# Seven block products in place of eight in the second input half of the second feed-forward parts

## The reference

```
def swiglu(x, w_in, w_out):
    gate, up = jnp.split(x @ w_in, 2, axis=-1)
    return (jax.nn.silu(gate) * up) @ w_out

x = x + 0.5 * swiglu(rmsnorm(x, p['ffn2_norm'][i]), p['ffn2_w_in'][i], p['ffn2_w_out'][i])
```

## Time and profile before

| | us |
|---|---|
| median of 3 runs (2357.9 to 2358.71) | 2358.68 |
| profiled execution, span from first to last instruction | 2357.9 |
| PE busy in it | 2332.7 |
| DVE busy | 1295.9 |
| ACT busy | 869.0 |
| POOL busy | 609.4 |

### The profile page before, as it was taken

How to read it: one execution, slowest core, us unless ns; L and a number is a source line. 1 busy time by engine, 2 the same in 40 slices (tenths; PEclk the granted TensorE clock), 3 DMA queues, 4 the chain that set the end, 5 groups by cost and what they waited for, 6 DMA issues and landing times.

```text
span 2357.9 us, 50146 instructions
## 1 busy us (share of the span) xinstructions
PE 2332.7 (99%) x21043; PEld 2270.3 (96%) x21043; DVE 1295.9 (55%) x1906; ACT 869.0 (37%) x1399; POOL 609.4 (26%) x591
## 2 busy tenths in 40 slices
PE   8999999999999999999999999999999999999999
PEld 8999999889979999999999999999999979999999
DVE  6653643964576443445543344577777666443443
ACT  4422333453233321322433233267775233321323
POOL 4779967331103000004111010432122102000003
PEclk9999999999999999999999999999999999999999
DMA  6455445553562333333543333233332653333332
GB/s 167 128 161 149 123 134 169 171 170 107 166 242 84 98 99 91 96 96 99 158 117 111 100 108 115 83 100 108 104 111 77 213 188 91 97 94 94 98 94 94
DMA packets 483707, 289.19 MB, mean 123 GB/s; under 512 B 22289, under 2 KB 466962, under 8 KB 482514
## 3 DMA queue, kind: packets, MB, share of 16 engines
q1 hardware_dynamic: 477856, 280.66, 40.4%
q0 software_dynamic: 560, 1.84, 0.6%
q10 hardware_dynamic: 5122, 4.25, 0.5%
HBM read 258.86 MB, written 27.85 MB: 122 GB/s over the span
## 4 chain that ended last, share of the span: by engine, by line
PE 90%; DVE 4%; POOL 2%; ACT 1%; issue 1%; DMA 1%; SPq 0%; DVEq 0%; POOLq 0%; ACTq 0%
PE lin L3021 51%; PE lin L3026 25%; PE mis L2512 4%; POOL sTmp L737 1%; PE mis L2650 1%; PE lin L2600 1%; PE lin L2762 1%; PE mis L2633 1%; PE lin L2757 1%; PE lin L2983 1%; POOL sGe L738 0%; DVE w_lo L1827 0%; POOL sFe L738 0%; PE lin L2650 0%; PE mis L2626 0%
## 5 line engine op out<-in xcount | busy, mean ns | idle before, releaser
L1827 DVE TENSOR_TENSOR w_lo<-raw,w_hi 128x1024 fp32r<-128x1024 f32 (+1 forms) x322 | 464.0, 1441 | 294.4 <-ACT w_hi L1330 293.7
L1330 ACT ACTIVATE w_hi<-raw 128x1024 fp32r<-128x1024 f32 (+1 forms) x328 | 365.1, 1113 | 314.2 <-PE lin L3026 244.4
L3021 PE MATMUL lin<-a_rear,w_hi 128*128 128x264 f32 x3552 | 455.6, 279 | 0.0
L3021 PE MATMUL lin<-a_front,w_hi 128*128 128x256 f32 x3552 | 451.5, 279 | 1.1 <-DVE a_rear L1840 0.7
L3021 PEld LDWEIGHTS lin<-a_rear,w_hi 128*128 128x128 f32 x3552 | 432.6, 188 | 0.0
L3021 PEld LDWEIGHTS lin<-a_front,w_hi 128*128 128x128 f32 x3552 | 424.4, 188 | 4.5 <-issue 1.8
L3026 PE MATMUL lin<-a_rear,w_lo 128*128 128x264 f32 x1776 | 245.1, 278 | 0.0
L3026 PE MATMUL lin<-a_front,w_lo 128*128 128x256 f32 x1776 | 240.5, 277 | 1.0 <-DVE w_lo L1827 1.0
L2391 DVE SCALAR_TENSOR_TENSOR xT<-lin,xT 128x520 f32<-128x520 f32 (+1 forms) x87 | 60.9, 700 | 322.8 <-PE lin L3026 322.1
L1063 POOL TENSOR_TENSOR acc<-xT 128x520 f32<-128x520 f32 x8 | 12.2, 1521 | 864.6 <-DVE xT L2391 836.6
L3026 PEld LDWEIGHTS lin<-a_rear,w_lo 128*128 128x128 f32 x1776 | 223.8, 188 | 0.0
(11 more groups left out here) (512 smaller groups left out, 3181.5 us busy)
## 6 DMA issues: line engine op xcount, KB each, us to landing
raw<-in_ffn_w_in_dram SPq DMA_DIRECT2D x176, 512.0 KB, 3.9
raw<-in_ffn_w_out_dram SPq DMA_DIRECT2D x64, 704.0 KB, 4.6
kc<-in_cache_mem_k_dram SPq DMA_DIRECT2D x32, 512.0 KB, 7.1
vc<-in_cache_mem_v_dram SPq DMA_DIRECT2D x16, 1024.0 KB, 9.1
raw<-in_hg_w_in_dram SPq DMA_DIRECT2D x32, 512.0 KB, 4.3
raw<-in_xattn_w_kv_dram SPq DMA_DIRECT2D x16, 512.0 KB, 4.4
raw<-in_s_w_glu_dram SPq DMA_DIRECT2D x16, 512.0 KB, 4.0
raw<-in_xattn_w_q_dram SPq DMA_DIRECT2D x16, 512.0 KB, 3.9
```

The costliest lines, as they stand in the source:

```text
L1330: act.activation(w_hi[:, j, 0:kt, :], raw[:, j, 0:kt, :], ACT.Copy).then_inc(hi_ready, 1)
L1827: dve.tensor_tensor(low_weights(n, j), raw[:, j, 0:kt, :], w_hi[:, j, 0:kt, :].bitcast(F32), ALU.subtract).then_inc(lo_ready, 1)
L3021: pe.matmul(lpart(j, half), high[:, k, :], (x_lo if u else x_hi)[half][:, k, :], start=start and u == 0 and k == 0, stop=False)
```

## The change

The input product of ffn2_in1 in both layers is computed by Winograd's form of Strassen's scheme. For one hidden tile the weights are a 2 x 2 matrix of blocks: row A1 is the gate column block, row A2 the value column block, and the second index is the half of the 1024 input features (KQ = 4 tiles of 8). The tokens are a 2 x 2 matrix too: input half by token half (HT = 260 columns). Seven block products of four weight tiles replace eight; four of them use sums of weight blocks (S1 to S4), four use sums of token blocks (T1 to T4). Each sum is again split into a high and a low part.

- In ffn2_in0 of the same part, hooks after pairs 1, 3, 5, 7 make the token blocks (`mixed`, with gain and rstd already in them) and after pairs 2, 4, 6, 8 their high (ACT) and low (DVE) parts. That stage is unrolled now. They lie over the space of the S5 tables and of the memory keys and values.
- In the last pair of out0, DVE also makes S1 to S4 for the first pair.
- In ffn2_in1, ACT, DVE and PE run `seven_products`, a written-out list of 11 pairs; SP's loop is as before. DVE's order decides when lo_ready rises: `low_22` raises it by 2 for the whole pair, and `low_11` raises a new semaphore, first_low. sum_raw, sum_hi and sum_lo have two buffers; raw, w_hi and w_lo still one.
- PE's seven products go to seven PSUM banks, in the order 1, 2, 4, 6, 5, 7, 3; DVE combines the banks into gate and value rows. rstd is no longer applied there.
- Three semaphores of the HGRN2 lower bound become one, and four spare ones go.

The new functions and their order, cut to what each engine issues:

```
    # tokens, DVE
+            def mixed(layer, k):
+                for name in ("B11", "B12", "B21", "B22"):
+                    m, cols = k + KQ * (name[1] == "2"), HALVES[name[2] == "1"]
+                    ins = dve.scalar_tensor_tensor(out=mix[name], in0=xT[:, m, cols], scalar=vec[:, row + m:row + m + 1],
+                                                   in1=rstd[:, cols], op0=ALU.mult, op1=ALU.mult)
+                step.link(ins)
+                step.link(dve.tensor_tensor(mix["T1"], mix["B12"], mix["B11"], ALU.subtract))
+                step.link(dve.tensor_tensor(mix["T2"], mix["B22"], mix["T1"], ALU.subtract))
+                dve.tensor_tensor(mix["T3"], mix["B22"], mix["B12"], ALU.subtract)
+                dve.tensor_tensor(mix["T4"], mix["B21"], mix["T2"], ALU.subtract).then_inc(combined, 1)
    # weights, DVE
+            def weight_sums(p, q, pair):
+                for j in range(2):
+                    dve.wait_ge(raw_arrived[j], 16 * (p + 1))
...
+                if pair == 0:
+                    step.link(dve.tensor_tensor(s["S1"], w["A21"], w["A22"], ALU.add))
+                    dve.tensor_tensor(s["S2"], s["S1"], w["A11"], ALU.subtract).then_inc(combined, 1)
+                else:
+                    dve.tensor_tensor(s["S3"], w["A11"], w["A21"], ALU.subtract)
+                    dve.wait_ge(combined, of_weights(q, 0))
+                    dve.tensor_tensor(s["S4"], w["A12"], s["S2"], ALU.subtract).then_inc(combined, 1)
    # ACT, seven_products
+                for i in range(FH):
...
+                        gate(i - 1)
+                    act.wait_ge(product_done, 4 * q + 1)
+                    act.activation(rows[:, ROW_P1], bank_p1, ACT.Copy).then_inc(product_kept, 1)
+                    if more:
+                        high_sums(q + 1, 0)
+                    split(p + 1, 0, n if more else n + 1)
+                    if i:
+                        hidden_hi(i - 1)
+                    if more:
+                        high_22(p + 1)
+                        high_sums(q + 1, 1)
    # DVE, seven_products
+                def low_22(p):
+                    dve.wait_ge(hi_ready, 2 * p + 2)
+                    dve.tensor_tensor(w_lo8[:, 1, KQ:KD, :], raw[:, 1, KQ:KD, :], w_hi[:, 1, KQ:KD, :].bitcast(F32),
+                                      ALU.subtract).then_inc(lo_ready, 2)
+                for i in range(FH):
...
+                        with_p3_p4(p - 1)
+                    if more:
+                        weight_sums(p + 1, q + 1, 0)
+                    if i:
+                        gated(i - 1)
+                    if more:
+                        weight_sums(p + 1, q + 1, 1)
+                        low_11(p + 1)
+                    u2 = with_p2_p6(q)
+                    if more:
+                        low_22(p + 1)
...
+                    if i:
+                        hidden_lo(i - 1)
+                    if more:
+                        low_sums(q + 1, 0)
+                    with_p5_p7(q, u2)
+                    if more:
+                        low_sums(q + 1, 1)
    # PE, seven_products: waits of product 4
+                    pe.wait_ge(hi_ready, 2 * p + 2)
+                    pe.wait_ge(used[0], p)
+                    high(bank_p4, w_hi[:, 1, KQ:KD], "T4")
+                    pe.wait_ge(lo_ready, 2 * p + 2)
+                    low(bank_p4, w_lo8[:, 1, KQ:KD], "T4").then_inc(product_done, 1)
```

More of the change, by code:

```diff
@@ L55, in link, with mark, after @@
         self.eng.wait_ge(self.sem, self.off + self.n)
+    def mark(self, ins):
+        ins.then_inc(self.sem, 1)
+        self.n += 1
+        return self.off + self.n
+    def after(self, mark):
+        self.eng.wait_ge(self.sem, mark)
     def loop(self, i, first, per):
@@ L511, in over_pairs, with seven, of_tokens, of_weights @@
         body(p0 + pairs - 1, pairs - 1, False, True)
+    def seven(n):
+        return n < len(ST) and ST[n][0] == "ffn2_in1"
+    COMBINED = KQ + 2 * FH
+    def of_tokens(layer, k):
+        return COMBINED * layer + k + 1
+    def of_weights(q, pair):
+        return COMBINED * (q // FH) + KQ + 2 * (q % FH) + pair + 1
+    MIX_RAW = {("ffn2_in0", l, 1 + 2 * k): k for l in range(DEPTH) for k in range(KQ)}
+    MIX_SPLIT = {("ffn2_in0", l, 2 + 2 * k): k for l in range(DEPTH) for k in range(KQ)}
     def chunk_after(n, j, last):
@@ L1764, in stream, with seven_products, high_22, high_sums @@
                 over_pairs(act, n, body, hook)
+            def seven_products(n):
+                p0, layer = first_pair[ST[n][:2]], ST[n][1]
+                def high_22(p):
+                    act.wait_ge(raw_arrived[1], 16 * (p + 1))
+                    act.wait_ge(chunk_done, 2 * p0)
+                    wait(act, product_done, 4 * (FH * layer + p - p0 - 1) + 2)
+                    act.activation(w_hi[:, 1, KQ:KD, :], raw[:, 1, KQ:KD, :], ACT.Copy).then_inc(hi_ready, 1)
+                def high_sums(q, pair):
+                    act.wait_ge(combined, of_weights(q, pair))
+                    blocks = slice(2 * pair, 2 * pair + 2)
+                    act.activation(sum_hi[:, q % FH % 2, blocks], sum_raw[:, q % FH % 2, blocks], ACT.Copy)\
+                        .then_inc(combined_high, 1)
+                def gate(i):
+                    act.wait_ge(used[0], p0 + i + 1)
+                    act.activation(rows[:, ROW_SILU], rows[:, ROW_GATE], ACT.Silu).then_inc(gate_out, 1)
+                def hidden_hi(i):
+                    act.wait_ge(used[1], p0 + i + 1)
+                    for out, cols in zip(f_hi, COLS):
+                        ins = act.activation(out[:, i, :], hidden_row[:, cols], ACT.Copy)
+                    ins.then_inc(h_hi_done, 1)
+                for i in range(FH):
+                    p, q, more = p0 + i, FH * layer + i, i + 1 < FH
+                    if i == 0:
+                        high_sums(q, 0)
+                        high_22(p)
+                        high_sums(q, 1)
+                    else:
[10 more added lines that the diff above has]
+                        high_sums(q + 1, 1)
+                gate(FH - 1)
+                hidden_hi(FH - 1)
             for n in range(len(ST)):
@@ L2355, in body @@
                                 split_part(p + 1, slice(0, FREE_LOW)).then_inc(lo_part, 1)
+                                if seven(n + 1):
+                                    weight_sums(p + 1, FH * layer, 0)
+                                    weight_sums(p + 1, FH * layer, 1)
                         if j == 0 and first and r is not None:
@@ L2399, in body @@
                                     gain_lo(m - 1, after)
-                            if late_low(n, j, last) and turns:
+                            if late_low(n, j, last) and turns and not seven(n + 1):
                                 split_part(p + 1, slice(FREE_LOW, KD)).then_inc(lo_ready, 1)
```

163 lines of the change are left out of this document (155 added, 8 removed).

## The result

| | before | after |
|---|---|---|
| median, us | 2358.55 (2357.9 to 2358.71, 4 runs) | 2385.97 (2383.44 to 2388.97, 4 runs) |
| span of the profiled execution | 2357.9 | 2387.2 |
| in1 of the second part, layer 0 / 1 | 121.73 / 121.72 | 134.37 / 135.30 |
| in0 of the second part, layer 0 / 1 | 122.44 / 122.44 | 122.85 / 122.91 |

The ratio is 1.0116 (95% interval 1.0102 to 1.0130): 27.4 us slower, where 25.6 were forecast (2384.3 us, range 2362 to 2404). The profiled execution is the slowest of the four. Its span is 29.3 us longer: 12.64 + 13.58 from the two rewritten stages, 0.41 + 0.47 from the two token stages, and 2.2 us from work ahead of them that the change does not touch and that varies between executions.

What follows compares the result with a forecast made beforehand. The prediction took the load loop of ffn2_in1 as the bound, 11.95 us per pair: 25.1 us for both stages plus 0.5 for the tokens, 2358.7 + 25.6 = 2384.3 us, range 2362 to 2404.

Steps and rivals of the forecast that it cites:

- the ring: In ffn2_in1, from both loads' landing through DVE and ACT to the next landing: 6.15 + 5.8 = 11.95 us per pair.
- the double load: In ffn2_in1, both raw loads are issued together behind low_22 and take 5.8 us to land; ends 5.0 and 6.5.
- The stage: ffn2_in1: first refill landed at 9.1, nine steps of 11.95, then 17.6 to the end: 134.3 us, 12.6 longer than before.
- The tail: End of ffn2_in1, from the landing for pair 10 to the stage's end: 17.6 us, with five last PE products at 1.38.
- this hand-over: From ffn2_in1 to the output part: costs nothing, as before.
- PE's price: In ffn2_in1, 84 matmuls per pair at 114.7 ns, 9.64 us; 31 us saved over 22 pairs if PE still bound.
- DVE's price: In ffn2_in1, DVE's instructions priced by distances between starts: 10.1 us of work per pair.
- Rival A: In ffn2_in1, the loads do not bind; DVE sets 10.45 to 10.5 us per pair, stage about 116, total 2347; chance 0.10.
- The tokens: Token sums and splits in ffn2_in0: 0.5 us in all, bounds 0 and 0.4 in each of 8.
- rival C: Clock halves after PE idles in ffn2_in1: single stretches cost nothing, staying at half gives about 2540 us; chance 0.03.

Runs made afterwards that it cites:

- experiment 1: Changed kernel, but every load in ffn2_in1 after the first pair brings 64 KB instead of 512 KB: 2351.89 us, ratio 0.9967 to the kernel before.
- experiment 2: Changed kernel, but in ffn2_in1 after the first pair the second load brings 256 KB instead of 512 KB: 2368.63 us, ratio 1.0037 to the kernel before.
- experiment 3: Changed kernel with low_11 and low_22 each raising lo_ready by 1, so each column is fetched once free: 2374.10 us, ratio 1.0064 to the kernel before.
- experiment 7: experiment 3 plus reordering: DVE's chain that frees raw first, ACT's splits before the high sums: 2358.61 us, ratio 0.9996 to the kernel before.
- experiment 4: Changed kernel without the four low-weight matmuls of product 5 in each pair: 2391.15 us, ratio 1.0144 to the kernel before.
- experiment 5: Changed kernel with one more 512-element DVE instruction per pair, behind the last low_sums: 2387.11 us, ratio 1.0117 to the kernel before.
- experiment 11: experiment 7 with the first pair's second column prepared before the stage and independent DVE work between dependent instructions: 2353.66 us, ratio 0.9978 to the kernel before.
- experiment 8: experiment 7 with the gating product moved from DVE to POOL: 2364.14 us, ratio 1.0015 to the kernel before.
- experiment 6: Kernel before plus only the token sums and their splits in unrolled ffn2_in0; ffn2_in1 keeps eight block products: 2361.38 us, ratio 1.0005 to the kernel before.

## Why the prediction was right, step by step

**The bound.** Right: it was the ring over the double load. Its links measured between the two S1 above, with the forecast's value behind each: S1 and link 0.73 (0.72), S2 and to ACT 0.72 (0.73), high_sums 0.97 (0.96), split and back 1.07 (1.09), low_11 1.15 (1.14), with_p2_p6 0.61 (0.62), low_22 to SP's issue 0.86 (0.89), together 6.11 against 6.15. From issue to S1 the double load took 5.97 in this pair and 5.88 in the one before (issue 955.77, S1 961.65) against 5.8. In these the landing itself took 5.87 and 5.79, and 0.1 from it to S1 was not in the sum; over the 20 double loads of both stages the landing has a median of 5.7. Experiments 1 and 2 show that the loads are in the ring, 3 and 7 that its order is, 4 and 5 that neither engine's work is.

**The stage.** The forecast was 9.1 + 9 x 11.95 + 17.6 = 134.3. Layer 0 has 8.91 + 9 x 11.84 + 18.92 = 134.37. That the sum meets it to 0.1 is luck, for two errors cancel: the rings are 0.11 shorter (their steps run from 11.60 to 12.08), 1.0 in nine. The tail is 1.3 longer: up to product 4 it is the 10.71 forecast (1066.91 less 1056.21 gives 10.70), but then the five products cost 7.15 instead of 6.9, the last of them ends 0.23 behind that, and PE idles 0.84 us before the output stage's first matmul. The forecast had put this hand-over at nothing, "as before". The profile names no releaser for it ("issue"), but the rows do. In the output stage `chunk` waits for used[0], which with_p3_p4 raises. In the last pair that instruction runs behind the last product, from 1074.33 to 1075.03, and PE starts at 1075.13. In the eleven traces with `seven_products`, in both layers, PE starts 0.10 us after its end. Before, chunk 0's bank was read while chunk 1 ran, and the earlier trace rows show no gap. Layer 1 is 0.9 longer than layer 0, 0.8 of it in the rings.

**PE's price.** Mis-sized: 114.7 ns a matmul was placed between the prices for 256 and 264 columns. It measured 1.43 / 12 = 119 ns, above both. In the changed kernel it took from PE's idle time, 1.8 us per pair (11.84 - 10.0) and not 2.3, but it is why the floor of a pair is 10.0 and not 9.64 us, and the most that PE could save is 1.04 us in each of 22 pairs, 23 us and not 31.

**DVE's price.** Right: 10.1 us of work was forecast (its terms add up to 10.18); in experiment 11, where one of the two 0.11 us links counted in it is gone, a pair is 10.00. Rival A's step of 10.45 to 10.5 is the 10.46 of experiment 1, but its total of 2347 was 5 too low against 2351.9: the stage took 118.0 and 118.3, not 116.

**The tokens.** Forecast 0.5 us in all, measured 0.41 + 0.47 in the two stages: 0.4 too little, within what the total can tell.

**The clock.** As rival C had it for single stretches: the clock fell to half after an idle, for about 3.4 us, once in layer 0 and three times in layer 1, and the ring covered it. The windows of the one in layer 0:

```profile
955.00:956.00 1.00, 1.00 (x5) 0.77 (x4) 1.00 (x2) 0.00 (x0) 0.00 (x0) 0.50 0.00 0
957.00:958.00 1.00, 1.00 (x8) 0.81 (x7) 0.97 (x3) 0.00 (x0) 0.00 (x0) 0.93 0.78 206
```

PE had waited 2.26 us at 953.18. The S1 steps around it, 11.98 and 12.08, stand within 0.25 us of the usual 11.83. The clock did not fall in each pair: of the eleven waits that PE ends between 953.18 and 1066.91 in layer 0, ten left it at full.

**The rest of the 27.4 us.** 25.6 were forecast. The 2.2 us of the profiled span that arise ahead of these stages are no effect of the change: other kernels with the same code there start the in0 stage at 752.9 to 755.1, this execution at 756.6.

## What to carry to other kernels

An algorithm that takes an eighth of the bound engine's work gave nothing here until the buffer that feeds it was freed early: follow from the release of a single buffer through its load back to the next release, and add that ring up before counting the saved work. Put what frees the buffer first in every engine's order, release it in the pieces in which it is loaded, and place independent instructions between dependent ones. When all that is done, sum each engine again at its measured prices; here both TensorE and VectorE ended at 10.0 us per pair, where 9.64 and 10.1 were forecast. Then look at the ends of the stage, which order within a pair does not touch: the best order gained 5 of the 23 us that TensorE's work shrank by. In layer 0 of experiment 11 PE still idles 3.8 us behind the first double load (950 to 956) and 0.84 us at the hand-over.

## What was not expected of the hardware

- A matmul with 260 columns costs 119 ns against 113 with 256 and 116 with 264. The price does not follow the width alone; these products differ from the rows before in their operands and banks too, and the reason stays open.
- A VectorE instruction with two SBUF inputs took 1.71 instead of 0.69 us beside a 1.31 us GpSimd instruction (experiment 8), so an idle GpSimd is no free place for elementwise work next to a full VectorE.
- The profile can put a wait down to "issue" though another engine ends it: the 0.84 us in which PE waited for DVE's last combination. The token kernel of experiment 6 passes from written-out code to a loop as well, after ffn2_in0, and its row shows no gap, so the form of the code is not what costs there.

```profile
877.75 2.20 PE L3327 MATMUL lin<-f_front,w_hi 128*128 128x256 f32 x18
```

- Two 512 KB loads issued 0.6 us apart both land within 6 us of the first issue, except where a transfer of instructions starts within 3.4 us of it: then 5.99 to 7.03 us (21 of 160, experiment 11). The ring of the changed order passes that on in full: 1.3 us more on the load is 1.3 us more on the step of 13.2 in experiment 4.
